# A narrow forgetting tile, keys written once, and a reordered program end in a two-layer encoder trunk

## What is computed

```python
h = h + 0.5 * rms_norm(swiglu(rms_norm(h, g[0]), ...), g[1])
proj = u @ w_in                                   # u = rms_norm(h, g[2])
qa, ka, va, us, qc, kc, vc, fc = split(proj)      # 512,128,128,256,256,256,256,4 columns
ya = swa_sink_attention(qa, ka, va, sinks, cos, sin)   # 8 query heads, 2 key heads
yb = s5_mixer(us, ...)
yc = fox_attention(qc, kc, vc, fc, fox_f_bias)    # cum = cumsum(log_sigmoid(fc + f_bias))
h = h + rms_norm(concat(norm(ya), norm(yb), norm(yc)) @ w_out, g[3])
h = h + 0.5 * rms_norm(swiglu(rms_norm(h, g[4]), ...), g[5])
```

## Time and profile before

| | us |
|---|---|
| median of three runs | 1875.81 |
| lowest, highest | 1875.55, 1876.25 |
| the profiled execution | 1874.11 |
| its span, first to last instruction | 1872.3 |

### The profile page before, as it was taken

One profiled execution on the slowest core, in us unless ns is written; L12 is line 12 of the kernel. 1 busy time (PEld: TensorE's weight loads), 2 busy tenths in 40 slices (PEclk: granted clock), 3 DMA queues, 4 the chain that ended last, 5 costly groups with the idle time before them and its releaser, 6 DMA issues.

```text
span 1872.3 us, 25256 instructions
## 1 busy us (share of the span) xinstructions
PE 1856.3 (99%) x9480; PEld 1534.4 (82%) x9480; DVE 986.5 (53%) x1350; ACT 710.3 (38%) x1115; POOL 202.3 (11%) x420
## 2 busy tenths in 40 slices
PE   9999999999999999999999999999999999999998
PEld 7888888888678888888888888889886888888887
DVE  6664433387757544432476544325877574444323
ACT  5333332255755333322253333223666453333321
POOL 3832000013100000000047200000130000000000
PEclk9999999999999999999999999999999999999999
DMA  6335343343223333343333443333511313333331
GB/s 197 101 103 146 95 119 93 85 144 102 57 68 91 98 93 101 95 121 94 100 93 99 108 132 113 107 95 104 161 51 53 113 57 101 93 98 114 97 93 45
DMA packets 332013, 188.61 MB, mean 101 GB/s; under 512 B 7028, under 2 KB 327512, under 8 KB 330904
## 3 DMA queue, kind: packets, MB, share of 16 engines
q1 hardware_dynamic: 325992, 168.60, 31.3%
q0 software_dynamic: 5824, 18.79, 3.3%
q10 hardware_dynamic: 112, 0.05, 0.0%
HBM read 175.72 MB, written 11.67 MB: 100 GB/s over the span
## 4 chain that ended last, share of the span: by engine, by line
PE 96%; DVE 2%; ACT 2%; issue 0%; DVEq 0%; ACTq 0%
PE ps L595 19%; PE ps L597 18%; PE ps L596 18%; PE ps L804 8%; PE ps L805 8%; PE ps L806 8%; PE ps L652 2%; PE ps L654 2%; PE ps L659 2%; PE ps L990 1%; PE ps L764 1%; PE ps L763 1%; PE ps L765 1%; PE ps L625 1%; PE ps L636 1%; PE ps L627 1%
## 5 line engine op out<-in xcount | busy, mean ns | idle before, releaser
L1677 DVE TENSOR_TENSOR wl<-raw,wh 128x1024 fp32r<-128x1024 f32 (+1 forms) x260 | 344.4, 1325 | 729.3 <-ACT wh L1175 728.0
L595 PE MATMUL ps<-xh,wh 128*128 128x512 f32 x1536 | 606.1, 395 | 2.2 <-ACT vc L1398 2.2
L597 PE MATMUL ps<-xh,wl 128*128 128x512 f32 x1536 | 598.2, 389 | 0.0
L596 PE MATMUL ps<-xl,wh 128*128 128x512 f32 x1536 | 597.9, 389 | 0.0
L1175 ACT ACTIVATE wh<-raw 128x1024 fp32r<-128x1024 f32 (+1 forms) x260 | 295.8, 1139 | 621.4 <-PE ps L806 324.6
L595 PEld LDWEIGHTS ps<-xh,wh 128*128 128x128 f32 x1536 | 288.4, 188 | 66.1 <-issue 4.8
L597 PEld LDWEIGHTS ps<-xh,wl 128*128 128x128 f32 x1536 | 288.3, 188 | 60.5
L596 PEld LDWEIGHTS ps<-xl,wh 128*128 128x128 f32 x1536 | 288.5, 188 | 60.0 <-issue 1.9
L804 PE MATMUL ps<-Hh,wh 128*128 128x512 f32 x638 | 248.4, 389 | 0.0
L806 PE MATMUL ps<-Hh,wl 128*128 128x512 f32 x638 | 248.2, 389 | 0.0
L805 PE MATMUL ps<-Hl,wh 128*128 128x512 f32 x638 | 248.2, 389 | 0.0
(11 more groups left out here) (390 smaller groups left out, 2020.0 us busy)
## 6 DMA issues: line engine op xcount, KB each, us to landing
raw<-in_ffn_gate SPq DMA_DIRECT2D x88, 512.0 KB, 3.8
raw<-in_ffn_up SPq DMA_DIRECT2D x88, 512.0 KB, 3.8
raw<-in_ffn_down SPq DMA_DIRECT2D x64, 704.0 KB, 4.5
raw<-in_w_in SPq DMA_DIRECT2D x28, 512.0 KB, 4.1
raw<-in_w_out SPq DMA_DIRECT2D x16, 512.0 KB, 3.6
xrow<-in_x SPq DMA_DIRECT2D x4, 512.0 KB, 7.2
ssm_t<-evict POOLq DMA_DIRECT2D x8, 256.0 KB, 3.6
ssm_v<-evict POOLq DMA_DIRECT2D x8, 256.0 KB, 3.5
```

Source lines behind the costliest of these rows:

```text
L595: pe.matmul(bank, w_tile(True, slot, kw), xh[:, kx, :], start=first, stop=False)
L596: pe.matmul(bank, w_tile(True, slot, kw), xl[:, kx, :], start=False, stop=False)
L597: return pe.matmul(bank, w_tile(False, slot, kw), xh[:, kx, :], start=False, stop=last)
L1677: V.tensor_tensor(w_low(slot, k0, nk), raw[:, slot4, 0:nk - k0, :], w_high(slot, k0, nk).bitcast(F32), ALU.subtract).then_inc(w_split, 1)
```

## The change

The tile fc reads only 32 of its 128 columns: ScalarE writes their high part in columns 96 to 127 of the weight tile, VectorE their low part in columns 64 to 95, and TensorE does two products a k-tile with 64 columns of weights instead of three. Rows 0 to 31 of the bank then hold the low part's share and rows 32 to 63 the high part's, and `forget` takes three steps. VectorE's low part of unit 7 comes ahead of `forget`, ScalarE's `forget` moves from the turn of va to that of qa0, and `forget_sum` from behind qa0 to behind qa1. The sum for the norm moves two k-tiles later within va. The keys are written once by VectorE and copied by ScalarE into the other halves. At the end TensorE sums the squares first and then turns the rows in order, and the last row block is stored in two halves.

```diff
+FC_ROWS = 2 * (P - CUM0)
+def narrow_from(s, i):
+    return CUM0 if s % 3 == 1 and i in (2, 3) else 0
@@ sync: the end
-            for t in range(TOK):
+            for t in range(TOK - 1):
                 sp.wait_ge(s_rowc, 2 * t + 2)
                 sp.dma_start(out[0, t * P:(t + 1) * P, :], ...
-            sp.wait_ge(s_out, 16 * TOK)
+            for half in range(2):
+                sp.wait_ge(s_rowc, 2 * TOK - 1 + half)
+                sp.dma_start(out[0, (TOK - 1) * P:TOK * P, half * SEQ:(half + 1) * SEQ],
+                             hrow[:, 2 * TOK - 2 + half, :]).then_inc(s_out, 16)
+            sp.wait_ge(s_out, 16 * (TOK + 1))
@@ tensor: unit_x
-                    if k == 3 and between is not None:
+                    if k == 5 and between is not None:
@@ tensor: first_four (all its products now go through this)
+                narrow = TILE["fc"] if s % 3 == 1 else None
+                def product(u, high, xt, k, cols_h, start, stop):
+                    if u != narrow:
+                        return pe.matmul(ps[u][:, cols_h], w_tile(high, cols[u][1], k), xt[:, k, cols_h], start=start, stop=stop,
+                                         skip_group_check=True)
+                    if high:
+                        return pe.matmul(ps[u][0:FC_ROWS, cols_h], w_tile(True, cols[u][1], k)[:, P - FC_ROWS:P], xt[:, k, cols_h],
+                                         start=start, stop=stop, skip_group_check=True)
@@ tensor: output_rows
-                pe.wait_ge(s_hcopy, 2 * TOK)
-                pe.wait_ge(yv, dn + 4)
-                for t in range(3):
-                    turn_y(t, 0)
                 pe.wait_ge(y_used, dn + KD + 1)
...
                 mm.then_inc(post_sum, 1)
+                pe.wait_ge(s_hcopy, 2 * TOK)
+                pe.wait_ge(yv, dn + 4)
+                turn_y(0, 0)
                 pe.wait_ge(y_used, dn + KD + 2)
-                for t in range(3):
+                turn_y(0, 1)
+                for t in range(1, 3):
+                    turn_y(t, 0)
                     turn_y(t, 1)
@@ tensor: scores
+                            pe.wait_ge(k_other, (l + 1) * 2)
...
-                                               kz[r, j // 2, k0:k0 + P], start=(c > 0), stop=True, skip_group_check=True)
+                                               kz[r, a ^ (j // 2), k0:k0 + P], start=(c > 0), stop=True, skip_group_check=True)
@@ scalar: split (split_ahead passes narrow_from(s, i) as c0)
-                act.activation(w_high(slot, k0, nk), raw[:, slot4, 0:nk - k0, :], ACT.Copy).then_inc(w_hi, 1)
+                act.activation(w_high(slot, k0, nk)[:, :, c0:P], raw[:, slot4, 0:nk - k0, c0:P], ACT.Copy).then_inc(w_hi, 1)
@@ scalar: mixer
+                def other_halves():
+                    act.wait_ge(qk_rdy, l * (1 + SWA_PAIRS) + 1)
+                    for a in range(2):
+                        act.activation(kz[64 * a:64 * a + 64, 1, :], kz[64 - 64 * a:128 - 64 * a, 0, :],
+                                       ACT.Copy).then_inc(k_other, 1)
...
                         swap(m, rotated)
                         rotated += 1
-                    if m == TILE["fc"] + 2:
+                        if rotated == 2:
+                            other_halves()
+                    if m == TILE["fc"] + 3:
                         forget()
@@ vector: low (low_ahead passes narrow_from(s, i) as c0)
-                V.tensor_tensor(w_low(slot, k0, nk), raw[:, slot4, 0:nk - k0, :],
-                                w_high(slot, k0, nk).bitcast(F32), ALU.subtract).then_inc(w_split, 1)
+                dst = w_high(slot, k0, nk)[:, :, P - FC_ROWS:CUM0] if c0 else w_low(slot, k0, nk)
+                V.tensor_tensor(dst, raw[:, slot4, 0:nk - k0, c0:P],
+                                w_high(slot, k0, nk)[:, :, c0:P].bitcast(F32), ALU.subtract).then_inc(w_split, 1)
@@ vector: mixer
-                    mlink(V.tensor_tensor(full[r, 1, :], ps[bank_of(m)[0]][r, :], rstd[r, :], ALU.mult))
+                    r, bank = slice(CUM0, P), ps[bank_of(m)[0]]
+                    mlink(V.tensor_tensor(full[r, 1, :], bank[0:FC_ROWS // 2, :], rstd[0:FC_ROWS // 2, :], ALU.mult))
+                    mlink(V.tensor_tensor(full[r, 0, :], bank[FC_ROWS // 2:FC_ROWS, :], rstd[FC_ROWS // 2:FC_ROWS, :], ALU.mult))
+                    mlink(V.tensor_tensor(full[r, 1, :], full[r, 1, :], full[r, 0, :], ALU.add))
...
-                    if u == 6:
+                    if u == 5:
                         low_unit(base + 7, in_slot(7))
...
-                        rotate(m, rotated, 1.0, [(kz[64 * a:64 * a + 64, kv, :], slice(64 * kv, 64 * kv + 64))
-                                                 for kv in range(2) for a in range(2)])
+                        rotate(m, rotated, 1.0, [(kz[:, 0, :], slice(0, P))])
...
-                    if m == TILE["fc"] + 3:
+                    if m == TILE["fc"] + 4:
                         forget_sum()
@@ vector: the end
-                    dve.wait_ge(s_row, half * 3 + t + 1 if t < 3 else 7 + half)
+                    dve.wait_ge(s_row, 2 * t + half + 1)
```

More of the change, by code:

```diff
@@ L425, in build @@
         qk_rdy = sem("rotated_tile_ready")
+        k_other = sem("keys_in_other_halves_ready")
         fox_rdy = sem("fox_q_or_k_ready")
@@ L611, in first_four @@
                 order = FIRST if s else FIRST0
+                narrow = TILE["fc"] if s % 3 == 1 else None
[6 more added lines that the diff above has]
+                                         start=start, stop=stop, skip_group_check=True)
+                whole = slice(0, SEQ)
                 if s:
@@ L623, in first_four @@
                                     pe.wait_ge(w_split, cols[u][0] + RAW_SLOTS + 1)
[L624 to L628, removed]
+                                product(u, True, xh, k, cols_h, first and k == 0, False)
+                                product(u, False, xh, k, cols_h, False, False)
                             if first and k == 0:
@@ L635, in first_four @@
                             for u in ALL4:
-                                pe.matmul(ps[u][:, cols_h], w_tile(True, cols[u][1], k), xl[:, k, cols_h],
-                                          start=False, stop=False, skip_group_check=True)
+                                product(u, True, xl, k, cols_h, False, False)
                 for step, (ks, us_) in enumerate(order):
@@ L650, in first_four @@
                         for u in us_:
[L651 to L655, removed]
+                            product(u, True, xh, k, whole, k == 0, False)
+                            product(u, False, xh, k, whole, False, False)
                         pe.wait_ge(x_rdy, xn * KD + k + 1)
                         for u in us_:
-                            mm = pe.matmul(ps[u][:, :], w_tile(True, cols[u][1], k), xl[:, k, :], start=False, stop=(k == KD - 1),
-                                           skip_group_check=True)
+                            mm = product(u, True, xl, k, whole, False, k == KD - 1)
                             if k == KD - 1:
@@ L1169, in ssm_functions, with split, split_unit @@
                 act.activation(identb[:, :], ident[:, :], ACT.Copy).then_inc(act_c, 1)
-            def split(n, q, slot4, slot, nk, occupant=2, k0=0):
+            def split(n, q, slot4, slot, nk, occupant=2, k0=0, c0=0):
                 act.wait_ge(landed[slot4], q * 16 + 16)
                 act.wait_ge(unit_done, n + SPLIT_SLOTS + 1 - occupant)
-                act.activation(w_high(slot, k0, nk), raw[:, slot4, 0:nk - k0, :], ACT.Copy).then_inc(w_hi, 1)
-            def split_unit(n, slot, nk=KD, occupant=2, k0=0):
-                split(n, n // 4, n % 4, slot, nk, occupant, k0)
+                act.activation(w_high(slot, k0, nk)[:, :, c0:P], raw[:, slot4, 0:nk - k0, c0:P], ACT.Copy).then_inc(w_hi, 1)
+            def split_unit(n, slot, nk=KD, occupant=2, k0=0, c0=0):
+                split(n, n // 4, n % 4, slot, nk, occupant, k0, c0)
             def split_ahead(s, i):
                 n, slot, k0, k1, since = ahead(s, i)
-                split_unit(n, slot, k1, since, k0)
+                split_unit(n, slot, k1, since, k0, narrow_from(s, i))
             def root(total, width, r, lns, ln_count, done):
@@ L1672, in ssm_inverse, with low, low_unit @@
                     link(V.tensor_scalar(nsinks[r, :, :], mine, -1.0, None, ALU.mult))
-            def low(n, slot4, slot, nk, k0=0):
+            def low(n, slot4, slot, nk, k0=0, c0=0):
                 dve.wait_ge(w_hi, n + 1)
-                V.tensor_tensor(w_low(slot, k0, nk), raw[:, slot4, 0:nk - k0, :],
-                                w_high(slot, k0, nk).bitcast(F32), ALU.subtract).then_inc(w_split, 1)
-            def low_unit(n, slot, nk=KD, k0=0):
-                low(n, n % 4, slot, nk, k0)
+                dst = w_high(slot, k0, nk)[:, :, P - FC_ROWS:CUM0] if c0 else w_low(slot, k0, nk)
+                V.tensor_tensor(dst, raw[:, slot4, 0:nk - k0, c0:P],
```

(11 more changed lines are left out.)

## The result

The changed kernel takes 1880.72 us (median of 10 runs, 1880.14 to 1882.97) against 1875.44 us before (10 runs): ratio 1.0031 [1.0023, 1.004], slower by about 0.3%. The forecast was 1876.7 us within 1872.4 to 1878.4, so the result is outside the range. The profiled execution took 1881.68 us with a span of 1879.9 us, one of the slower of the ten; it is 7.6 us above the span before, of which 0.54 us is a later start of the first product (9.71 against 9.19 us).

What follows compares the result with a forecast made beforehand. TensorE, busy in 99% of the span, and a chain of waits through ScalarE and VectorE to the third attention item bound it. 1.12 + 0.89 - 1.15 = +0.86 us on 1874.11, median 1.70 above: 1876.7 us, range 1872.4 to 1878.4.

Steps and rivals of the forecast that it cites:

- Where TensorE meets it: Third attention item: +1.12 us in layer 0, +0.89 in layer 1; TensorE's saved 3.7 us become two waits.
- Products saved: Forgetting tile on TensorE: one product fewer per k-tile at the same pace, 1.86 us a layer, 3.7 in both.
- The sum for the norm: TensorE's sum of squares for the mixer's norm: starts at 402.75; rstd 0.27 us earlier in layer 0, 0.5 in layer 1.
- VectorE's idle time ahead of unit 9's low part: Layer 0, after qa0's rotation: VectorE idle for 2.3 us until ScalarE has made unit 9's high part.
- Key copies: ScalarE behind the swap of qa0: two copies at 0.6 us each, with ends at 0.4 and 0.8.
- The rotation of qa2: VectorE, layer 0: starts at 430.93 without idle time ahead, +1.39 us before the norm's 0.27 us shift.
- Third item: Scores of the third attention item on TensorE: later by 1.12 us in layer 0 and 0.89 in layer 1.
- The end: Program's end: row sums ahead of the turns bring VectorE's first step 1.15 us earlier; the halved last store brings nothing.
- (1): ScalarE steps do not hold VectorE up; its path shortens by its work alone: 1872.5 us, 20%.
- (2): TensorE alone bounds, so the products saved count in full: -4.6 us, 1871.2 us, 6%.
- (3): Narrow products save nothing, so the norm's sum comes 1.36 us later: +4.4 us, 1880.2 us, 5%.
- (4): Added delay is absorbed in the items behind it, and only the program's end counts: 1874.7 us, 9%.

Runs made afterwards that it cites:

- late forget steps: Changed kernel with ScalarE's three forget steps behind the swap of qa3 and forget_sum behind the second item's maxima, key copies left in place: 1870.99 us, 0.9975.
- the filled runs: Changed kernel with 16 or 8 unused products of 384 columns ahead of TensorE's wait for the third attention item: 1876.67 us and 1876.78 us.
- 8 fillers: Changed kernel with 8 unused products of 384 columns ahead of TensorE's wait for the third attention item: 1876.78 us, 1.0008.
- the short delay: Kernel before with VectorE repeating the last step of qa3's rotation twice, no product changed: 1879.69 us, 1.0022.
- late copies: Changed kernel with only the two key copies moved, from behind the swap of qa0 to ahead of the swap of qa2: 1876.9 us, 1.0007.
- the long delay: Kernel before with VectorE repeating the last step of qa3's rotation four times, no product changed: 1885.06 us, 1.0052.

## Why the prediction was wrong

**The failed step** is the last sentence of "Where TensorE meets it": "The saved 3.7 us become two waits of about 2.8 us." The waits are there, 2.80 and 2.81 us. They were priced at their length. But behind them the granted clock stands at half its full level for 6.8 us, and what TensorE does meanwhile takes nearly twice as long (0.43 us a product and not 0.227): +2.45 and +2.83 us in the profiled execution, about 4 us in the medians (1880.72 less 1876.67 with TensorE kept at work). Without it the time is 1876.67 us, 1.6 us above the kernel before in the same runs, where the terms of the sum made 0.86; the two meet at 1876.7 only because the median then at hand (1875.81) was 0.7 us higher than the later ones.

A row of before had the hint. The window of the earlier trace rows, 5 us without a TensorE instruction, was read for its DMA share. Its granted clock is 0.71: half level for 2.9 of the 5 us, from 1868.4 on, with TensorE silent since its last turns, started at 1863.16 and over at 1865.54: 2.9 us of silence and then the fall. A change that makes silences of 2.8 us had to be held against it.

**The terms, one by one.**
- Products saved: pace and count right. Where nothing waits they give most of their 3.7 us: with the late forget steps the time is 4.5 us below before, of which 1.1 to 1.5 are the end, so 3.0 to 3.4.
- The sum for the norm: 403.33 less 0.54 is 402.79, forecast 402.75. In layer 1 it is 1331.01, and less the 4.47 us inherited 1326.54, forecast 1326.24: 0.2 us won and not 0.5.
- VectorE's idle time ahead of unit 9's low part: 2.42, forecast 2.3. Key copies 1.29 us, forecast 1.2. The rotation of qa2 has no idle time ahead of it, as forecast; it comes 1.49 us later than before, forecast 1.12 (1.39 less 0.27). Of the missing 0.37 about 0.15 is there by unit 7's low part; the rest is small steps between ScalarE and VectorE.
- Third item: +1.48 and +1.40, forecast +1.12 and +0.89. This is the 0.87 us by which the sum's terms were too low; the filled runs (1.6 us above before) bear it out.
- The end: -1.22, forecast -1.15; halves nothing, as forecast.

**The rivals.** (1) fell: ScalarE's steps do hold VectorE up (2.42 us). (2), TensorE alone, at 1871.2, came true only once those steps and `forget_sum` were moved (1870.6). (3) named about the measured time, 1880.2, for a cause that did not occur: a narrow product keeps the pace. (4) fell: nothing behind the item gives the delay back. The chance of slower by over 0.2%, 5%, had no case in it in which a wait costs more than its length.

The Trainium skill (TensorE: Matmul & The Clock Gate, HAM oscillation) prices a low clock at the time spent at half rate times one half. The rows agree when only the time that TensorE works is counted: 3.4 us at work give 1.7, measured 1.57 to 1.60; 5.35 of 6.8 us give 2.7, measured 2.45; 6.2 of 6.8 give 3.1, measured 2.83. With the spacings measured here, 0.43 against 0.227 us, the share lost is 0.47 and not one half, and the three come to 1.6, 2.5 and 2.9.

**Still open:** what decides whether a wait of 1.5 us brings a fall. It was none behind the one of 1.49 us with 8 fillers, one behind the two of 1.52 in the short delay, two behind the two of 1.72 and 1.69 with late copies; and the silence of 2.21 us ahead of the first product brought none. The kernel before, whose trace has none of these waits, has a spread of its own: of its 83 executions in the three sets of experiments, 62 had a mean granted clock of 0.999 or 1.0 and took 1874.3 to 1876.6 us, and 21 had 0.998 or 0.997 and took 1875.9 to 1878.5. Where in the span their clock was low is not known, since none of them has a trace.

The two lengths of a low stretch have a pattern in the seven traced falls at the third item. Where the clock fell inside the wait (both layers of the changed kernel, layer 0 of the long delay) it stayed low for 6.8 us; where it fell 0.3 to 1.0 us after TensorE was back at work (late copies in both layers, short delay, layer 1 of the long delay) for 3.4 us. Why a fall comes in one place or the other is open.

## What to carry to other kernels

Price a new silence of an engine that sets the time not at its length alone: where the engine is TensorE, ask what the granted clock does in rows where it is silent (here a window at the program's end), and add about half of the time that it then works at the low level. When work is taken off such an engine, look at what fills its place; if other engines can't deliver sooner, the saved work is worth nothing, and may be worth less than nothing. Steps moved on a helper engine belong behind the last one that the next unit waits for: moving the three forget steps (2.1 us on ScalarE) and the `forget_sum` that hangs on them (3.1 us on VectorE) made the difference between 1880.7 and 1871.0 us.

## What the runs showed of the hardware

- In otherwise full work silences of TensorE of 1.69 to 3.05 us brought the granted clock from its full level to half (six of six); of three of about 1.5 us one did. One of 2.21 us ahead of the first product did not.
- The low stretches were 6.8 us long where the clock fell during the silence and 3.4 us where it fell after it.
- Filling such a silence with products whose results nobody reads made the kernel about 4 us faster.
- At half level the spacing of products of 512 columns was 0.43 us and not 0.23.
- Products with 64 columns of weights keep the pace of those with 128.
